# A new opening and first stage with projections one tile ahead, in a hybrid-mixer inference step

## The chip, the cores and the metric

One Trainium2 chip, one of its cores. The metric is the device time of one execution in microseconds; the kernel before takes 2571.53 us as the median of three runs (2570.34 to 2575.14). One execution was profiled: 2571.76 us of device time, of which the profile's span, from the first to the last instruction, covers 2569.9 us.

## What is computed

1024 latent and 256 context tokens of 1024 channels pass one layer: a modulated RMSNorm, an input projection of 56 column tiles of 128, three token mixers in parallel (Hyena long convolution, FNet, RG-LRU), a gated merge, an output projection, a second norm and a SwiGLU feed-forward. Cut to what the change touches:

```
mod = silu(c) @ w_ada + b_ada              # shift, scale, gate of both norms, for latent and context
h   = rmsnorm(x, n1) * (1 + sc1) + sh1
u   = h @ w_in                             # tiles: 12 Hyena, 4 FNet, then pairs (recurrent input, gate), 24 gates
k   = sin(freq * (sin(freq * (feats @ fw1 + fb1)) @ fw2 + fb2)) @ fw3 * decay     # Hyena filters, 8 chunks
kf  = rfft(k);   v, x1, x2 = depthwise_conv(u_hy, 3 taps)
xr  = depthwise_conv(u_rx, 4 taps)
r, i = sigmoid(xr @ w_r + b_r), sigmoid(xr @ w_i + b_i)     # per block of 128 channels, two directions
log_a = -8 * r * softplus(-lam);  h = scan(exp(log_a), sqrt(1 - a*a) * i * xr)
```

## The kernel before, in words

The program is written by hand for five engines, each with its own instruction list; semaphores order them. The order of the work is the order in each list. Activations lie with channels on the 128 partitions and the 1280 tokens along the free axis, in three pieces: 512 and 512 latent tokens, 256 context tokens. All products keep full precision: a weight tile is split by POOL into a rounded high part and a remainder (`split`, L798 and L801), `h` likewise into `h_hi` and `h_lo`, and `split_product` (L840 to L842) adds three products. One projection tile is 8 channel blocks x 3 pieces x 3 products into PSUM banks 0 to 2 (`projection_tile`). The other five banks, 3 to 7, are handed out in turn to all other products (`MixUnits`; `mix_done` and `mix_free` count them).

The stages that the change touches:

**Opening** (to the first projection). PE computes the filter network's two small layers (L893, L900) over 1280 positions, with 64 hidden channels. VectorE (DVE) takes each layer's argument into the range of the sine (`reduce_angle`, L1684 to L1688) and ScalarE (ACT) takes the sine (L1280, L1296). The second layer is computed twice, into both halves of the partitions (`h2f`). ACT squares the eight channel blocks of x (L1270), DVE sums them (L1677), and ones-products give the mean square of each token (L909); its inverse root goes onto diagonals (L1730) and is spread over the partitions by three more products (L917); DVE multiplies x by it (L1751). In between PE makes four rows of the modulation (`ada_row_unit`, L877, 16 products with 32 output channels each in four column groups), one after the other: each row is copied by ACT (L1288 and the line before it), turned into columns by PE (`ada_turn_unit`, L886) and added to its bias by DVE (L1736) before ACT may copy the next, since all share one buffer. DVE and ACT then make `h_hi` and `h_lo` block by block (L1785 to L1802), and PE's first projection waits for each block. The softplus of the decay parameters (three small parts on DVE, `softplus`, with an Exp and a Ln on ACT in between, L1275 and L1277) runs during the squares.

**First stage**: 16 projection tiles (12 Hyena, 4 FNet) and 8 filter chunks in eight passes (`l1_pass`; seven in a loop, the last apart). After `projection_tile(0)` and the filter taps of chunk 0 (`taps_units`, L945), pass i issues on PE: an ada row (L877), three products of the filter's spectrum (`fwd_unit`, L930) which wait for DVE's even part (`fa_ready`), projection tile 2i+1, a sum, three more spectrum products which wait for DVE's odd part, the turn, the taps of chunk i+1, and projection tile 2i+2. For each Hyena or FNet tile ACT writes a base (`conv_base`, L1331) and DVE adds two neighbours (`conv_sides`, L1814 to L1818) and frees the three banks. DVE further makes the taps (`make_taps`, L1853), their sums and the first stage of a transform (`first_stage`, L219 to L231).

**Second stage**: eight chunks of FNet and recurrent work. For chunk n PE issues projection tiles 16+2n and 17+2n, then waits for `xr_ready` and issues 12 products (L1023); ACT copies the first tile into the padded buffer `rin` (L1342), and DVE convolves it into `xr` (`conv_chunk`, L1828 and L1833), which also waits for that chunk's constants `rpack`. SP loads `rpack` of chunk 0 (L652) only after all eight filter chunks are stored (L643, L651).

SP issues every DMA from one list; `load_ahead(t, slot)` loads tile t+2 once tile t is split.

Of the kernel before, what the change touches and what calls it, by code (L numbers as in the profile page):

```python
# [14 lines left out]
P = 128  # L15
# [25 lines left out]
def u_made(n, by_act):  # L41
    return U_BY_ACT[:n + 1].count(by_act)

# [246 lines left out]
def build_program(nc, dr):  # L290

    ctx = ExitStack()
    with ctx:
# [11 lines left out]
        feats = sb(st, "feats", [FILT_EMB, T])  # L305
        h1f = sb(st, "h1f", [FILT_HID, T])
        arg, turns = sb(st, "arg", [P, T]), sb(st, "turns", [P, T])
# [24 lines left out]
        h2f = filt_ada[:, :]  # L332
# [17 lines left out]
        f_w2 = sb(st, "f_w2", [FILT_HID, P])  # L350
# [182 lines left out]
        FILT_UNIT = (0, 1, 2, 4, 5, 6)  # L533
        SQUARES_UNIT = 3
        ROW_UNIT = tuple(range(7, 7 + 2 * ROWS_FIRST, 2))
        TURN_UNIT = tuple(range(8, 8 + 2 * ROWS_FIRST, 2))
        u_setup = MixUnits([0] * MIX_BANKS, 6 + 1 + 2 * ROWS_FIRST)
# [50 lines left out]
        def _(sp):  # L588
# [37 lines left out]
            def l1_pass(i, last):  # L626
                load_ahead(2 * i, 0)
                if not last:

                    sp.wait_ge(taps_ready, i + 1)  # L630
                    load_taps(i + 1)
                sp.wait_ge(hy_conved, 2 * i + 2)
                sp.dma_start(dr["hy_s"][2 * i], hout[0][:]).then_inc(hy_stored[0], 16)
                load_ahead(2 * i + 1, 1)
                if not last:

                    sp.wait_ge(ada_row_ready, i + (ROWS_FIRST + 1))
                    for g in range(2):
                        sp.dma_start(ada_w[g][:], dr["w_ada"][2 * i + (ADA_FIRST + 2 + g)]).then_inc(ada_in[g], 16)
                sp.wait_ge(hy_conved, 2 * i + 3)  # L640
                sp.dma_start(dr["hy_s"][2 * i + 1], hout[1][:]).then_inc(hy_stored[1], 16)
# [193 lines left out]
        def _(pe):  # L835
# [53 lines left out]

            pe.wait_ge(filt1_in, 32)  # L890
            for j, (a, e, _) in enumerate(PIECES):
                out, done = mix_unit(u_setup, 0, FILT_UNIT[j])
                mm(out[0:FILT_HID, 0:e - a], f_w1[:, :], feats[:, a:e], start=True, stop=True).then_inc(done, 1)  # L893

            pe.wait_ge(consts_set, 3)
            pe.wait_ge(filt_in, 32)
            pe.wait_ge(sin_ready, 1)
            for j, (a, e, _) in enumerate(PIECES):
                out, done = mix_unit(u_setup, 0, FILT_UNIT[3 + j])
                mm(out[:, 0:e - a], f_w2[:, :], h1f[:, a:e], start=True, stop=True).then_inc(done, 1)  # L900
            pe.wait_ge(csilu_set, 2)
            pe.wait_ge(vec_in, 16)
            for r in range(ROWS_FIRST):
                ada_row_unit(u_setup, 0, ROW_UNIT[r], [2 * r, 2 * r + 1], 16)
                if r == 0:
                    out, done = mix_unit(u_setup, 0, SQUARES_UNIT)
                    pe.wait_ge(x_sq_summed, KD - 1)
                    for tile in range(NT):
                        ins = mm(out[:, 2 * tile:2 * tile + 2], x_sq_sum[:, tile * P:(tile + 1) * P], ones[:, 0:2],  # L909
                                 start=True, stop=True)  # L910
                    ins.then_inc(done, 1)
                ada_turn_unit(u_setup, 0, TURN_UNIT[r], r + 1, 0, 512)
                if r == 1:

                    pe.wait_ge(diag_ready, 1)
                    for b, (a, e, _) in enumerate(PIECES):
                        mm(ps[b][:, 0:e - a], ones[:],  # L917
                           rstd_diag[:, a // P:e // P, :].rearrange("p t m -> p (t m)"),
                           start=True, stop=True).then_inc(proj_done[b], 1)
# [15 lines left out]
            def taps_units(units, it, j0, loads):  # L935

                pe.wait_ge(w3_in, loads)
                for group in ((0, 1), (2, 3), (4,)):
                    banks_of = [mix_unit(units, it, j0 + j) for j in group]
                    for s in range(2):  # L940
                        for half, j in enumerate(group):
                            out, done = banks_of[half]
                            tile = 2 * j + s
                            rows = slice(half * FILT_HID, (half + 1) * FILT_HID)
                            ins = mm(out[:, s * 256:(s + 1) * 256], h2f[rows, tile * P:(tile + 1) * P], w3[rows, :],  # L945
# [4 lines left out]
            def l1_pass(i, units, it, last):  # L950
# [5 lines left out]
                projection_tile(2 * i + 1, 1)  # L956
# [54 lines left out]
            with pe.Fori(0, KD // 2) as m:  # L1011
                for s in range(2):
                    n = 2 * m + s
                    projection_tile(2 * n + L2_TILE0, 0)
# [10 lines left out]
                    if s == 0:  # L1025
                        fnet_channels(m)

# [206 lines left out]
        def _(act):  # L1234
# [19 lines left out]
            def take_filter(layer):  # L1254
                rows = P if layer else FILT_HID
# [4 lines left out]
                for j, (a, e, _) in enumerate(PIECES):  # L1260
                    src, free = take_mix(u_setup, 0, FILT_UNIT[3 * layer + j])
                    fn(arg[0:rows, a:e], src[0:rows, 0:e - a], ACT.Identity, bias=f_bias[0:rows, layer:layer + 1],
                       scale=f_vec[0:rows, 2:3]).then_inc(free, 1)

            for k in range(KD):
# [7 lines left out]
                if k == 3:  # L1273
                    act.wait_ge(sp_ready, 1)
                    fn(sp_w[:, 2, :], sp_w[:, 1, :], ACT.Exp).then_inc(sp_act, 1)  # L1275
                    act.wait_ge(sp_ready, 2)
                    fn(sp_w[:, 4, :], sp_w[:, 3, :], ACT.Ln).then_inc(sp_act, 1)  # L1277
                if k == KD - 3:
                    act.wait_ge(arg_ready, 1)
                    fn(h1f[:, :], arg[0:FILT_HID, :], ACT.Sin).then_inc(sin_ready, 1)  # L1280
            take_filter(1)
            act.wait_ge(consts_set, 3)
            for r in range(ROWS_FIRST):
                src, free = take_mix(u_setup, 0, ROW_UNIT[r])
                act.wait_ge(mod_ready, r)
                own(fn(ada_row[:, :], src[:, :], ACT.Copy))
                act.sem_inc(free, 1)
                act.sem_inc(ada_row_ready, 1)  # L1288
                if r == 0:
                    src, free = take_mix(u_setup, 0, SQUARES_UNIT)  # L1290
                    own(fn(rstd_col[:, :], src[:, 0:2 * NT], ACT.Sqrt, bias=eps[:, 0:1], scale=1.0 / D))
                    act.sem_inc(free, 1)
                    act.sem_inc(rms_ready, 1)
                if r == 1:
                    act.wait_ge(arg_ready, 2)
                    fn(h2f[:, :], arg[:, :], ACT.Sin).then_inc(sin_ready, 1)  # L1296
# [9 lines left out]
            act.wait_ge(proj_done[2], 1)  # L1306
            fn(rstd_ctx, ps[2][:, 0:CTX], ACT.Copy).then_inc(proj_free[2], 1)
# [48 lines left out]
            def l1_pass(i, units, it, last):  # L1356

                conv_base(2 * i, 0)
# [8 lines left out]
                conv_base(2 * i + 1, 1)  # L1367
# [10 lines left out]

            taps_squares(0)
# [4 lines left out]
            act.wait_ge(rin_zero, 1)  # L1384
# [988 lines left out]
```

## Time and profile before

| | us |
|---|---|
| median of three runs | 2571.53 |
| the profiled execution | 2571.76 |
| its span | 2569.9 |
| PE busy | 2479.5 (96%) |
| DVE busy | 1460.8 (57%) |
| POOL busy | 696.0 (27%) |
| ACT busy | 620.9 (24%) |

PE is TensorE's matmuls. A busy share is an average over the stages; the idle tenth of a stage has to be looked up where it stands. The granted clock is a mean of 0.983 over the span; 1.0 is 2.4 GHz and 0.5 is 1.2 GHz.

### The profile page before, as it was taken

What the parts mean: (1) busy time and instruction counts of PE and PEld (TensorE: products, weight loads), DVE (VectorE), ACT (ScalarE), POOL (GpSimd) and SP (SyncE); (2) the same over time, 40 slices, a digit from 0 to 9 for tenths busy, and PEclk for the clock granted to TensorE, in tenths of its full rate; (3) what the DMA queues carried; (4) which work ended last, traced back from release to release, by engine and by line L of the source; (5) the groups of instructions that cost most, each with busy time, mean ns of one, the idle gap of its engine ahead of it and who ended that gap; (6) DMA issues with size and microseconds to landing.
All of it is one profiled execution on the core that took longest, in us unless ns stands there. A gap on an engine that the chain in (4) does not pass through costs nothing. (4 is left out here: it accounts for less than half of the span.)

```text
span 2569.9 us, 34710 instructions
## 1 busy us (share of the span) xinstructions
PE 2479.5 (96%) x13478; PEld 2102.7 (82%) x13478; DVE 1460.8 (57%) x2697; ACT 620.9 (24%) x889; POOL 696.0 (27%) x300
## 2 busy tenths in 40 slices
PE   5799999999997999999999999999999999999997
PEld 2588888877876888888878878888888888888886
DVE  5878786678777676777763474633223322333236
ACT  4422222575753222222210012300000000000004
POOL 1011111223121222222333460442314331342220
PEclk8799999999998999999999999999999999999999
DMA  7244443111232222222453250111101010110002
GB/s 303 84 162 157 161 157 135 65 55 51 82 122 104 101 100 100 100 100 107 155 212 126 88 193 20 50 49 34 34 31 49 33 49 16 49 49 33 25 25 83
DMA packets 53755, 234.26 MB, mean 91 GB/s; under 512 B 6131, under 2 KB 8755, under 8 KB 48068
## 3 DMA queue, kind: packets, MB, share of 16 engines
q1 hardware_dynamic: 53700, 233.54, 25.2%
q8 instruction: 34, 0.56, 0.1%
q14 instruction: 21, 0.17, 0.0%
HBM read 178.98 MB, written 54.53 MB: 91 GB/s over the span
## 5 line engine op out<-in xcount | busy, mean ns | idle before, releaser
L840 PE MATMUL ps<-h_hi,w_hi 128*128 128x512 f32 (+1 forms) x2112 | 762.1, 361 | 13.5 <-DVE h_lo L1799 6.3
L841 PE MATMUL ps<-h_lo,w_hi 128*128 128x512 f32 (+1 forms) x2112 | 751.0, 356 | 0.0
L842 PE MATMUL ps<-h_hi,w_lo 128*128 128x512 f32 (+1 forms) x2112 | 750.9, 356 | 0.0
L798 POOL TENSOR_TENSOR w_hi<-w_raw,zero_col 128x1024 fp32r<-128x1024 f32 x96 | 206.4, 2150 | 1583.9 <-PE ps L842 1385.4
L840 PEld LDWEIGHTS ps<-h_hi,w_hi 128*128 128x128 f32 x2112 | 401.3, 190 | 78.8 <-issue 14.6
L842 PEld LDWEIGHTS ps<-h_hi,w_lo 128*128 128x128 f32 x2112 | 401.1, 190 | 57.1
L841 PEld LDWEIGHTS ps<-h_lo,w_hi 128*128 128x128 f32 x2112 | 401.5, 190 | 56.4 <-issue 0.2
L2151 DVE TENSOR_TENSOR a<-sil,ps 128x512 f32<-128x512 f32 (+1 forms) x66 | 39.5, 599 | 504.1 <-PE ps L842 501.7
L801 POOL TENSOR_TENSOR w_lo<-w_raw,w_hi 128x1024 fp32r<-128x1024 f32 x96 | 270.1, 2813 | 7.5
L2174 DVE SCALAR_TENSOR_TENSOR x<-ps,mod,x 128x512 f32<-128x512 f32 (+1 forms) x264 | 172.3, 661 | 98.1 <-PE ps L842 97.6
L841 PE MATMUL ps<-h_lo,wf_hi 128*128 128x512 f32 (+1 forms) x624 | 224.4, 360 | 0.0
L840 PE MATMUL ps<-h_hi,wf_hi 128*128 128x512 f32 (+1 forms) x624 | 223.1, 358 | 0.0
L842 PE MATMUL ps<-h_hi,wf_lo 128*128 128x512 f32 (+1 forms) x624 | 221.8, 355 | 0.0
L1568 ACT ACTIVATE sil<-ps 128x512 f32<-128x512 f32 (+1 forms) x66 | 34.7, 527 | 752.0 <-PE ps L842 751.8
L840 PE MATMUL ps<-act_hi,wf_hi 128*128 128x512 f32 (+1 forms) x528 | 187.2, 355 | 0.6 <-DVE act_lo L2157 0.6
L842 PE MATMUL ps<-act_hi,wf_lo 128*128 128x512 f32 (+1 forms) x528 | 186.9, 354 | 0.0
L841 PE MATMUL ps<-act_lo,wf_hi 128*128 128x512 f32 (+1 forms) x528 | 186.9, 354 | 0.0
L798 POOL TENSOR_TENSOR wf_hi<-w_raw,zero_col 128x1024 fp32r<-128x1024 f32 x48 | 94.8, 1974 | 181.2 <-PE ps L842 181.2
L840 PEld LDWEIGHTS ps<-h_hi,wf_hi 128*128 128x128 f32 x624 | 117.2, 188 | 20.4 <-issue 0.2
L841 PEld LDWEIGHTS ps<-h_lo,wf_hi 128*128 128x128 f32 x624 | 117.5, 188 | 18.3 <-issue 0.2
L842 PEld LDWEIGHTS ps<-h_hi,wf_lo 128*128 128x128 f32 x624 | 117.1, 188 | 18.6
L801 POOL TENSOR_TENSOR wf_lo<-w_raw,wf_hi 128x1024 fp32r<-128x1024 f32 x48 | 116.0, 2418 | 3.8
(277 smaller groups left out, 3506.2 us busy)
## 6 DMA issues: line engine op xcount, KB each, us to landing
w_raw<-in_weights SPq DMA_DIRECT2D x146, 512.0 KB, 3.5
ada_w<-in_w_ada SPq DMA_DIRECT2D x18, 1024.0 KB, 8.1
scratch_gate_s<-g_st SPq DMA_DIRECT2D x24, 640.0 KB, 3.3
side<-scratch_gate_s SPq DMA_DIRECT2D x24, 640.0 KB, 4.0
scratch_k_s<-kstage SPq DMA_DIRECT2D x8, 1536.0 KB, 6.6
hy_k<-scratch_k_s SPq DMA_DIRECT2D x8, 1536.0 KB, 8.5
scratch_hy_s<-hout SPq DMA_DIRECT2D x16, 640.0 KB, 3.2
ada_early<-in_w_ada SPq DMA_DIRECT2D x6, 1024.0 KB, 22.2
```

Source lines behind the costliest of these rows:

```text
L798: nc.gpsimd.tensor_tensor(hi[:], w_raw[slot % 2][:], zero_col[:].to_broadcast([P, D]), ALU.add).then_inc(pool_step, 1)
L801: nc.gpsimd.tensor_tensor(lo[:], w_raw[slot % 2][:], hi[:].bitcast(F32), ALU.subtract).then_inc(split_done, 1)
L840: mm(out, w_pair[0], x_pair[0], start=first, stop=False)
L841: mm(out, w_pair[0], x_pair[1], start=False, stop=False)
L842: return mm(out, w_pair[1], x_pair[0], start=False, stop=last)
L1568: fn(sil[n % 2][:, 0:e - a], ps[b][:, 0:e - a], ACT.Silu).then_inc(f_free[b], 1)
L2151: tt(a32[n % 2][:, 0:e - a], sil[n % 2][:, 0:e - a], ps[ub][:, 0:e - a], ALU.mult).then_inc(f_free[ub], 1)
L2174: stt(x1[:, m, a:e], ps[b][:, 0:e - a], mod[:, 5 * KD + m, seq:seq + 1], x1[:, m, a:e], ALU.mult, ALU.add).then_inc(f_free[b], 1)
```

## The change

- The filter network runs on 768 columns in place of 1280: the positions are put into two halves of the partitions (`HALF_TILES`: six tiles of 128 positions each, the two context tiles in both), so `h1f`, `arg`, `turns` and `h2f` shrink to 768 columns and use all 128 partitions. Each layer is two pieces (512 and 256) x two halves, a half to each 64 output partitions.
- In the opening's order DVE sums all squares first and reduces the first angle then; the mean-square products come ahead of the second layer. The four ada rows get a buffer each (`ada_rows`), the four turns share one bank, and one DVE addition takes all four. Two rows' products follow the spreading products, then two turns, the last row, two turns.
- The softplus moves from the opening to the end of the first stage, on DVE and on ACT.
- Projections of the first stage run one tile ahead: `projection_tile(1)` follows the taps of chunk 0, pass i computes tiles 2i+2 and 2i+3, and the last pass computes tile 16, the recurrent input of chunk 0, in its middle and none at its end. ACT copies it into `rin` there, after DVE has zeroed the edges there. Bases, sides, loads and stores move with their tiles; one store comes ahead of the passes.
- The second stage's first pair of chunks is written out ahead of its loop, without tile 16.

```diff
+HALF_TILES = ((0, 1, 4, 5, 8, 9), (2, 3, 6, 7, 8, 9))
+HALF_T = 6 * P
+HALF_PIECES = [(0, 512), (512, HALF_T)]
...
             def l1_pass(i, last):                                  # SP
-                load_ahead(2 * i, 0)
+                load_ahead(2 * i + 1, 1)
...
-                sp.wait_ge(hy_conved, 2 * i + 2)
-                sp.dma_start(dr["hy_s"][2 * i], hout[0][:]).then_inc(hy_stored[0], 16)
-                load_ahead(2 * i + 1, 1)
+                sp.wait_ge(hy_conved, 2 * i + 3)
+                sp.dma_start(dr["hy_s"][2 * i + 1], hout[1][:]).then_inc(hy_stored[1], 16)
                 if not last:
+                    load_ahead(2 * i + 2, 0)
...
             load_taps(0)
+            load_ahead(0, 0)
+            sp.wait_ge(hy_conved, 2)
+            sp.dma_start(dr["hy_s"][0], hout[0][:]).then_inc(hy_stored[0], 16)
...
+            def filter_layer(layer, w_at, rows_at):                # PE
+                for j, (a, e) in enumerate(HALF_PIECES):
+                    out, done = mix_unit(u_setup, 0, FILT_UNIT[2 * layer + j])
+                    for half in range(2):
+                        rows = slice(half * FILT_HID, (half + 1) * FILT_HID)
+                        ins = mm(out[rows, 0:e - a], w_at(rows), rows_at(half, rows, a, e), start=True, stop=True)
+                    ins.then_inc(done, 1)
...
+            filter_layer(1, lambda rows: f_w2[rows, :], lambda half, rows, a, e: h1f[rows, a:e])
+            row_product(0)
+            pe.wait_ge(diag_ready, 1)
...
+            row_product(1)
+            row_product(2)
+            row_turn(0)
+            row_turn(1)
+            row_product(3)
+            row_turn(2)
+            row_turn(3)
...
                 for j in range(3):                                 # PE, l1_pass
                     fwd_unit(units, it, 1 + j, range(4 * j, 4 * j + 4), False, f_a, fwd)
-                projection_tile(2 * i + 1, 1)
+                projection_tile(2 * i + 2, 0)
...
                     taps_units(units, it, 9, 16 * i + 32)
-                    projection_tile(2 * i + 2, 0)
+                    projection_tile(2 * i + 3, 1)
             projection_tile(0, 0, h_ready)
             taps_units(u_taps, 0, 0, 16)
+            projection_tile(1, 1)
...
-                    projection_tile(2 * n + L2_TILE0, 0)           # PE, l2_pair
+                    if not (first and s == 0):
+                        projection_tile(2 * n + L2_TILE0, 0)
...
-                conv_base(2 * i + 1, 1)                            # ACT, l1_pass
+                if not last:
+                    conv_base(2 * i + 2, 0)
+                else:
+                    act.wait_ge(rin_zero, 1)
+                    into_padded(L2_TILE0 + 1, rin)
...
+            for k in range(1, KD):                                 # DVE
+                sum_square(k)
             reduce_angle(0)
...
+            conv_sides(0, 0)
             make_taps(u_taps, 0, 0, 16)
             even_stage()
...
             l1_pass(7, u1_last, 0, True)
+            for part in range(3):
+                softplus(part)
```

## Rows read from the trace of the kernel before

**Rows 1.** Waits of PE: line, releaser, us in total, times, longest.
```profile
PE ps L930 <- DVEq L1897: 12.9, 1, 12.9
```

**Rows 2.** Timeline of PE: start, us, instructions, [idle before <- releaser].
```profile
28.77 4.60 PE L900 MATMUL ps<-h1f,f_w 64*128 64x512 f32 x6 [16.44 <-ACT h1f L1280]
...
39.02 1.86 PE L886 MATMUL ps<-vec,ada_row 128*128 128x2 f32 x8 [0.41 <-ACTq L1292]
40.82 3.64 PE L877 MATMUL ps<-ada_early,csilu 128*32 128x256 f32 x32
...
47.08 4.61 PE L917 MATMUL ps<-rstd_diag,ones 128*128 128x512 f32 x6
...
55.89 1.93 PE L877 MATMUL ps<-ada_early,csilu 128*32 128x256 f32 x32
58.75 1.02 PE L886 MATMUL ps<-vec,ada_row 128*128 128x2 f32 x8 [0.93 <-ACTq L1288]
63.94 0.76 PE L840 MATMUL ps<-h_hi,w_hi 128*128 128x512 f32 x1 [4.17 <-DVE h_lo L1799]
...
90.42 4.37 PE L945 MATMUL ps<-w,filt_ada 64*128 64x256 f32 x20 [1.01 <-DMA w<-in_w]
94.72 1.93 PE L877 MATMUL ps<-ada_w,csilu 128*32 128x256 f32 x32
109.56 6.84 PE L930 MATMUL ps<-f_a,fwd 128*128 128x128 f32 x40 [12.90 <-DVEq L1897]
...
154.46 4.73 PE L930 MATMUL ps<-f_a,fwd 128*128 128x128 f32 x40
```

**Rows 3.** Stretches: us, then PE, PEld, DVE, ACT, POOL busy, granted clock, DMA share, GB/s.
```profile
45.00:50.00 5.00, 4.62 (x12) 3.10 (x13) 0.99 (x3) 2.67 (x3) 4.92 (x3) 0.50 0.98 411
54.00:56.00 2.00, 1.07 (x12) 1.08 (x16) 0.05 (x2) 0.60 (x1) 0.00 (x0) 1.00 0.02 4
90.00:92.00 2.00, 1.57 (x8) 1.32 (x10) 0.00 (x0) 0.00 (x0) 0.00 (x0) 0.50 0.93 291
```

**Rows 4.** Timeline of DVE in the opening and the first passes.
```profile
12.53 1.49 DVE L1677 TENSOR_TENSOR x_sq_sum<-x_sq_sum,x_sq 128x1280 f32<-128x1280 f32 x1 [4.15 <-ACT x_sq L1270]
...
14.78 0.82 DVE L1684 TENSOR_SCALAR turns<-arg 64x1280 f32<-64x1280 f32 x1 [0.25 <-DVE sp_w L1698]
...
16.48 3.00 DVE L1687 SCALAR_TENSOR_TENSOR arg<-turns,arg 64x1280 f32<-64x1280 f32 x2
...
61.40 0.17 DVE L1736 TENSOR_TENSOR mod<-ps,vec 128x8 f32<-128x8 f32 x1
...
93.33 4.04 DVE L1853 TENSOR_TENSOR taps<-ps,decay 128x256 f32<-128x256 f32 x10 [4.98 <-DMA decay<-in_decay]
...
153.53 1.28 DVE L1814 SCALAR_TENSOR_TENSOR hout<-ps,vec,hout 128x1023 f32<-128x1023 f32 x1 [1.22 <-ACT hout L1335]
```

**Rows 5.** The tile x_in to 110 us: its DMAs (first and last start), time to landing.
```profile
L606 SPq DMA_DIRECT2D x_in<-in_x x7: 432/445/814, 4.1 to 7.6; - x7
...
DMA to landing us min/median/max: 6.4/9.9/13.1
```

**Rows 6.** Timeline at the end of the first stage: DVE and PE.
```profile
451.33 8.77 DVE L1833 SCALAR_TENSOR_TENSOR xr<-rin,rpack,xr 128x1024 f32<-128x1024 f32 x6
...
434.67 0.95 PE L886 MATMUL ps<-vec,ada_row 128*128 128x2 f32 x8
...
463.15 8.75 PE L1023 MATMUL ps<-xr,rpack 128*128 128x512 f32 x24
```

**Rows 7.** There: SP's issue, the landing of rpack's two loads, L1833's durations (ns).
```profile
441.12 0.34 SPq L652 DMA_DIRECT2D rpack<-in_rpack  x1
...
DMA to landing us min/median/max: 2.8/6.9/11.1
...
L1833 DVE SCALAR_TENSOR_TENSOR xr<-rin,rpack,xr x6: 472/1284/3302, 451.3 to 459.6; 128x1024 f32<-128x1024 f32 x3, 128x256 f32<-128x256 f32 x3
```

**Rows 8.** Timeline of POOL there.
```profile
453.19 2.89 POOL L798 TENSOR_TENSOR w_hi<-w_raw,zero_col 128x1024 fp32r<-128x1024 f32 x1 [18.76 <-DMA w_raw<-in_weights]
```

More of the change, by code:

```diff
@@ L890, in _ @@
             pe.wait_ge(filt1_in, 32)
-            for j, (a, e, _) in enumerate(PIECES):
-                out, done = mix_unit(u_setup, 0, FILT_UNIT[j])
-                mm(out[0:FILT_HID, 0:e - a], f_w1[:, :], feats[:, a:e], start=True, stop=True).then_inc(done, 1)
+            filter_layer(0, lambda rows: f_w1[:, :], lambda half, rows, a, e: feats[:, half * HALF_T + a:half * HALF_T + e])
             pe.wait_ge(consts_set, 3)
+            out, done = mix_unit(u_setup, 0, SQUARES_UNIT)
+            pe.wait_ge(x_sq_summed, KD - 1)
@@ L896, in _ @@
+            for tile in range(NT):
+                ins = mm(out[:, 2 * tile:2 * tile + 2], x_sq_sum[:, tile * P:(tile + 1) * P], ones[:, 0:2],
+                         start=True, stop=True)
+            ins.then_inc(done, 1)
             pe.wait_ge(filt_in, 32)
             pe.wait_ge(sin_ready, 1)
-            for j, (a, e, _) in enumerate(PIECES):
-                out, done = mix_unit(u_setup, 0, FILT_UNIT[3 + j])
-                mm(out[:, 0:e - a], f_w2[:, :], h1f[:, a:e], start=True, stop=True).then_inc(done, 1)
+            filter_layer(1, lambda rows: f_w2[rows, :], lambda half, rows, a, e: h1f[rows, a:e])
@@ L1259, in take_filter, with take_row @@
                 act.wait_ge(f_bias_set, 1)
[L1260 to L1263, printed above, removed]
+                for j, (a, e) in enumerate(HALF_PIECES):
+                    src, free = take_mix(u_setup, 0, FILT_UNIT[2 * layer + j])
+                    fn(arg[:, a:e], src[:, 0:e - a], ACT.Identity, bias=f_bias[:, layer:layer + 1],
+                       scale=f_vec[:, 2:3]).then_inc(free, 1)
+            def take_row(r):
+                src, free = take_mix(u_setup, 0, ROW_UNIT[r])
+                own(fn(ada_rows[r][:, :], src[:, :], ACT.Copy))
+                act.sem_inc(free, 1)
+                act.sem_inc(ada_row_ready, 1)
             for k in range(KD):
@@ L1406, in take_fnet_tokens, with l2_pair @@
                     fn(dst, src, ACT.Copy).then_inc(free, 1)
-            with act.Fori(0, KD // 2) as m:
+            def l2_pair(m, first):
                 for s in range(2):
                     n = 2 * m + s
-                    act.wait_ge(xr_ready, n + 1)
-                    into_padded(2 * n + (L2_TILE0 + 1), rin)
+                    if not (first and s == 0):
+                        act.wait_ge(xr_ready, n + 1)
+                        into_padded(2 * n + (L2_TILE0 + 1), rin)
                     if s == 1:
@@ L1679, in reduce_angle @@
             def reduce_angle(layer):
-                rows = P if layer else FILT_HID
-                for j in range(3):
-                    mix_taken(u_setup, 0, FILT_UNIT[3 * layer + j])
-                x, n = arg[0:rows, :], turns[0:rows, :]
+                for j in range(2):
+                    mix_taken(u_setup, 0, FILT_UNIT[2 * layer + j])
+                x, n = arg[:, :], turns[:, :]
                 own(ts(n, x, 1.0 / (2 * math.pi), ROUND, ALU.mult, ALU.add))
@@ L1873, in l1_pass @@
                 dve.sem_inc(fa_ready, 1)
-                conv_sides(2 * i + 1, 1)
+                if not last:
+                    conv_sides(2 * i + 2, 0)
+                else:
+                    zero_edges()
                 ada_add(units, it, 8, 2 * i + ADA_FIRST, 4)
@@ L1879, in l1_pass, with zero_edges @@
                 own.restart()
+            def zero_edges():
+                for a, e in ((0, PAD_LAT), (PAD_LAT + LAT, PAD_CTX), (PAD_CTX + CTX, PAD_T)):
+                    own(nc.vector.memset(rin[:, a:e], 0.0))
+                dve.sem_inc(rin_zero, 1)
             def sum_squares(i):
```

162 lines of the change are left out of this document (78 added, 84 removed).

## Prediction

> **What bounds the kernel now.** The page first: PE is busy for 96% of the span, so time can be won only where PE stands still, or where its work waits in a chain of other engines. The waits of PE come next. In the whole first stage there is one wait for another engine, 12.9 us for DVE's even part before the first pass [rows 1]; in the passes that follow PE never waits. The timeline of PE [rows 2] shows the rest: 16.4 us of idle before the filter's second layer at 28.8, small products in a chain of copies to 59.8, 4.2 us of idle, and the first projection at 63.94. What ended last before that projection is the chain row product, ACT copy, turn, DVE addition (61.40, [rows 4]), the norm's scale, `h_hi`, `h_lo`. From there to 89.2 PE is fed block by block by DVE, and that pace is not changed. So there are three places: the path to 63.94, the hole before 109.56, and the passage to the second stage, where today PE goes from the last turn through tiles 16 and 17 to 463.15 [rows 6] with no wait in that view.
>
> **The change part by part: the opening.** x decides its head. The last of its loads is issued at 7.6 and may land 13.1 us later [rows 5], at 20.7. The DVE sums, undisturbed by angle and softplus, follow the loads: one square, about 1.3 us (the 1280-column sine and square are alike), and one sum, 1.49 [rows 4], give 23.5; the sum chain by itself, 12.53 + 7 x 1.49 = 23.0, is no later. The angle on 768 columns: the three scalar instructions fall from 0.82 to about 0.55 and the two fused ones from 1.5 to about 0.95 [rows 4], scaled with 0.15 us fixed each, 3.5 in all: 27.0. ACT's table load lies ahead of its wait, as the opening's others do. The sine, about 0.8, gives 28.0, with one hop 28.2. Before, the second layer began at 28.77: doing the angle last costs nothing, because the sums end 9 us earlier.
>
> The second layer took 4.60 us for 1280 columns [rows 2], 3.6 ns each. After, it has 512 + 256 columns for each of two halves. Side by side the halves cost 768 x 3.6 = 2.8 us, one after another 5.5. Nearest is the row of the taps: 10 products of 256 columns on alternating 64-row halves took 4.37 us [rows 2], 1.7 ns a column, and half of that lies at a granted clock of 0.50 [rows 3]: halves overlap there. I take 2.8: 31.0. The squares' products (2.4 us) lie in PE's idle time before the sine, and their root, on ACT right after the sine, gives the diagonals at 31.5.
>
> The Trainium skill, in "TensorEngine Tiling (Array Packing)", Restrictions and Gotchas, says that different row tiles can't use one PSUM bank at the same time. The taps' halves go to two banks and the new layer's two halves to one, so by the page this layer takes 5.5 us; no row of this trace has two row halves on one bank.
>
> Row product 0 follows: 3.0 at the low clock, 34.0. The three spreading products, 4.61 [rows 2]: 38.6. DVE scales two pieces from 36 to 46, beside this. Then PE has rows 1 and 2, turns 0 and 1, row 3, turns 2 and 3, and waits for no copy: a buffer each, and turns 0 to 2 have another product between copy and use. The last turn's copy hides behind turn 2. The cost hangs on the clock. The granted clock was 0.50 from 45 to 50 and 1.00 at 54 [rows 3]; the full 128x128 spreading products lay in between. After that a row took 1.93 and a turn 1.02, before it 3.64 and 1.86 [rows 2]. I take the same here, the clock rising behind the spreading products: 2.4 + 1.9 + 2 x 1.0 + 1.9 + 2 x 1.0 and 0.3 of hops = 10.5, so 49.1. From the addition to the first projection passed 63.94 - 61.40 = 2.54: 51.7, against 63.94. Gain 12.2. At the low clock throughout it is 3 x 3.6 + 4 x 1.86 = 18.2 and 59.4: gain 4.6. The weights' split on POOL (42 to 51) now overlaps DVE's scaling, which reads PSUM; the same pair overlapped before without slowing, so nothing. Ada loads landed by 41 and row 3 starts at 45.
>
> **The first stage.** In the old clock, from 89.2. `conv_sides(0)` now goes ahead of `make_taps` on DVE. It takes 3.5 us and starts at 90.0, when the base is made; make_taps began at 93.33, held by the decay's load [rows 4], so it is moved by 0.3 at most. Bank release at 93.6 comes before the taps' end at 94.8. PE then has tile 1: a tile is 13.8 us (435.6 to 463.15 for tiles 16 and 17, [rows 6], halved), to 108.6, and the ada row, 1.93, to 110.5, where today it stands still until 109.56. DVE's even part is ready at 109.8. So PE no longer waits, and the spectrum products, at a clock that has not fallen, take 4.73 and not 6.84 [rows 2]: tile 2 starts at 115.3 where tile 1 started at 116.15. A whole tile is done for nothing and 0.8 us are gained besides. Should the clock stay low for the tile's first 5 us, 2.5 us go.
>
> In the passes tile, base, sides, loads, stores and splits move by one tile together, and each engine has the same order as before. DVE keeps its room: in pass 1 it waits 1.22 us for ACT's base [rows 4], and PE takes the even part 2 us after it was made (154.46, [rows 2]). Nothing is gained or lost. The loads, stores and the wait for the second conv move on SP's queue in the same step; the store put ahead of the passes costs one issue of 0.3, and no tile waits for it. In the last pass tile 16 takes the place of 15; zeroing the edges, 0.3 us, lies in DVE's idle time.
>
> **The passage.** PE ends the last turn at 435.5 [rows 6] and now has only tile 17, to 449.3. Before, tiles 16 and 17 hid the making of xr. `rin` is filled by 430. The softplus on DVE and ACT starts at 435.9 and needs two table loads of 1.28 and some 3 us of small instructions: done by 440.8, with k_scale. What comes last is rpack: issued 441.12, once the last filter chunk is stored, and landed 2.8 us later [rows 7], at 443.9. The softplus is hidden with 3 us to spare. conv_chunk(0) took 10.1 us, its two largest parts drawn out to 3.3 and 2.1 us against 1.28 and 0.47 [rows 7], when POOL split tile 18 (453.19, [rows 8]). It now lies before that split, and undisturbed is 1.17 + 3 x 1.77 = 6.5: xr at 450.5. With the wait, PE starts the 12 products at 450.7, 1.4 us of new idle, where before it was 463.15 [rows 6]. With the 0.8 from the first pass, which moves the whole chain: gain 13.2.
>
> The FNet's first stage on DVE is late next: its input lands at 451.8, it takes 4, and POOL's split now falls on it, costing by the loss above up to 3.7: 459.5, and PE ends the 12 products (8.75, [rows 6]) at 459.4. So 0 to 2 us. The Trainium skill, in "SBUF — State Buffer", Who interferes with whom, has the pair as a lock held for a whole instruction; the rows agree in kind (3.3 and 2.1 us), and by it DVE could lose both of POOL's instructions, 5.3 us, and PE 1.7. Later stages are ordered by PE and don't change.
>
> **The sum.** 12.2 + 13.2 = 25.4 us off the profiled execution's own 2571.76 (span 2569.9 and 1.9 around it), which lies 0.2 above the median of 2571.53: 2546.3. I add 0.7 for the FNet stage: **2547**.
>
> **The rivals.** A. The two halves of the layer run one after another: 2.7 us more, 2550. For it: two row halves on one bank, which no row shows. B. The clock does not rise behind the spreading products, since the rows around them use few columns: 7.6 us more, 2554.5. For it: the second layer's 4.60 us did not raise it before. Against: one run of spreading products did. C. The passage is later than worked out: rpack lands late, or DVE meets a split: 3.7 to 5 us more, 2551. D. The extra tile waits for the sides behind DVE, or tile 16's place frees nothing: the hole stays and only the opening gains, 2571.8 - 12.2 = 2559.5; the change would not do what it says, but the bank's release before the taps' end speaks against it. E. Slower: in every pass DVE's sums and transform meet a split by POOL that now falls elsewhere. Each split costs DVE 3.7 us by the rows; two a pass are 7.4, less the room of 2.0, 5.4 over eight passes 43: 2547 + 43 = 2590. It decides from a delay of 5.1 us a pass on (25 / 8 + 2.0). Against it: POOL's split waits for the tile's end in both orders, so it stays where it was.
>
> **How the numbers follow.** Forecast 0.47, A 0.17, B 0.13, C 0.12, D 0.05, E 0.03, and 0.03 for no change to speak of. The first four, with 2543 to 2549 for the forecast's own spread, hold 0.89; a range from 2543 to 2557 takes B in and leaves out D, E and the tails, about 2 in 10. A change under 0.2% (5.1 us) can't be told from none here. Faster 0.93, same 0.04, slower 0.03.
>
> **What would show it.** First projection near 51.7 and PE's clock at 1.00 by 42; the second layer at 2.8 us; no wait of PE for L1897's successor, and tile 1 right behind the taps; one wait of 1 to 2 us before the 12 products, with rpack as what came last for DVE; L1833 without a 3.3. The prediction is wrong if PE's first projection is later than 58, or if waits of PE turn up inside the passes.

## The result, and the profile after

| | us |
|---|---|
| before, median of 4 runs | 2570.94 (2570.18 to 2575.14) |
| after, median of 4 runs | 2552.05 (2550.76 to 2560.04) |
| ratio | 0.9929, 95% interval 0.9916 to 0.9942 |
| after, the profiled execution | 2560.04, span 2558.2 |

The change is worth 18 to 19 us, 0.7%. 2547 was forecast, with a range of 2543 to 2557. The profiled execution after is the slowest of its four; a second profile of the same kernel, below, has a span of 2551.6. So this first profile shows larger losses than the second.

The timeline of PE after. The first seven lines answer to the opening [rows 2], the next two to the first pass, the last two to the passage [rows 6].

```profile
25.61 4.40 PE L929 MATMUL ps<-ones,x_sq_sum 128*128 128x2 f32 x20 [13.81 <-DVE x_sq_sum L1727]
30.09 2.82 PE L904 MATMUL ps<-h1f,f_w 64*64 64x512 f32 x8
32.84 2.74 PE L885 MATMUL ps<-ada_w,csilu 128*32 128x256 f32 x32
35.51 2.42 PE L942 MATMUL ps<-rstd_diag,ones 128*128 128x512 f32 x6
37.86 3.66 PE L885 MATMUL ps<-ada_early,csilu 128*32 128x256 f32 x64
45.19 1.96 PE L917 MATMUL ps<-vec,ada_row 128*128 128x2 f32 x16
53.19 0.76 PE L848 MATMUL ps<-h_hi,w_hi 128*128 128x512 f32 x1 [6.04 <-DVE h_lo L1846]
...
79.62 5.49 PE L979 MATMUL ps<-w,filt_ada 64*128 64x256 f32 x20 [1.49 <-DMA w<-in_w]
...
102.81 4.73 PE L963 MATMUL ps<-f_a,fwd 128*128 128x128 f32 x40
...
441.31 8.86 PE L1060 MATMUL ps<-xr,rpack 128*128 128x512 f32 x24 [0.62 <-DVEq L1883]
455.03 10.19 PE L1029 MATMUL ps<-fn_ch,fn_a 128*128 128x256 f32 x32 [4.86 <-issue]
```

The last line's products in the kernel before, from its timeline of PE, right behind the 12 products and without a wait:

```profile
471.74 7.07 PE L994 MATMUL ps<-fn_ch,fn_a 128*128 128x256 f32 x32
```

Read it by its shifts. The first projection comes 10.7 us earlier (63.94 to 53.19). The 12 recurrent products come 21.8 us earlier (463.15 to 441.31), with the hole of 12.9 us gone and a wait of only 0.6 us in the passage. Then, within one step, 4.9 us of idle ahead of the FNet products, and these take 10.2 us where they took 7.1: of 21.8 us 13.6 are left. The span is 11.7 us shorter, so some 2 us more go later: PE's waits at the output projection (the releasers now L2118 and L2127) are 8.4 us together against 6.2.

DVE and POOL side by side show what both losses are. First the timeline of DVE after, at the norm's start and in the passage:

```profile
42.34 4.87 DVE L1791 TENSOR_TENSOR x_in<-x_in,ps 128x512 f32<-128x512 f32 x8 [0.21 <-DVE x_in L1791]
47.43 0.19 DVE L1797 TENSOR_TENSOR mod<-ps,vec 128x32 f32<-128x32 f32 x1 [0.22 <-DVE x_in L1791]
47.86 1.96 DVE L1805 SCALAR_TENSOR_TENSOR norm_a<-mod,vec 128x8 f32<-128x8 f32 x2 [0.24 <-DVE mod L1797]
49.97 2.34 DVE L1832 TENSOR_SCALAR u_t<-x_in,norm_a,mod 128x512 f32<-128x512 f32 x1 [0.16 <-DVE norm_a L1805]
...
434.91 1.14 DVE L1875 TENSOR_SCALAR xr<-rin,rpack 128x1024 f32<-128x1024 f32 x2 [3.02 <-DMA rpack<-in_rpack]
436.09 5.11 DVE L1880 SCALAR_TENSOR_TENSOR xr<-rin,rpack,xr 128x1024 f32<-128x1024 f32 x6
...
444.34 2.18 DVE L226 TENSOR_TENSOR fn_a<-fn_c 128x128 f32<-128x128 f32 x2
...
446.78 2.44 DVE L226 TENSOR_TENSOR fn_c<-fn_c 128x128 f32<-128x128 f32 x1
449.14 1.98 DVE L223 TENSOR_TENSOR fn_c<-fn_c 128x128 f32<-128x128 f32 x1
...
451.24 2.43 DVE L226 TENSOR_TENSOR fn_a<-fn_c 128x128 f32<-128x128 f32 x1
...
454.61 0.28 DVE L226 TENSOR_TENSOR fn_a<-fn_u 128x128 f32<-128x128 f32 x1
```

and the timeline of POOL after, in the same places:

```profile
43.41 1.89 POOL L806 TENSOR_TENSOR w_hi<-w_raw,zero_col 128x1024 fp32r<-128x1024 f32 x1 [42.15 <-DMA w_raw<-in_weights]
...
47.70 1.89 POOL L806 TENSOR_TENSOR w_hi<-w_raw,zero_col 128x1024 fp32r<-128x1024 f32 x1
49.67 2.36 POOL L809 TENSOR_TENSOR w_lo<-w_raw,w_hi 128x1024 fp32r<-128x1024 f32 x1
...
444.40 1.97 POOL L806 TENSOR_TENSOR w_hi<-w_raw,zero_col 128x1024 fp32r<-128x1024 f32 x1 [39.15 <-DMA w_raw<-in_weights]
446.45 2.62 POOL L809 TENSOR_TENSOR w_lo<-w_raw,w_hi 128x1024 fp32r<-128x1024 f32 x1
449.04 1.94 POOL L806 TENSOR_TENSOR w_hi<-w_raw,zero_col 128x1024 fp32r<-128x1024 f32 x1
451.05 2.48 POOL L809 TENSOR_TENSOR w_lo<-w_raw,w_hi 128x1024 fp32r<-128x1024 f32 x1
```

A DVE instruction of 0.28 us, of which the transform is made, ends when the POOL instruction that ran beside it ends: 446.78 + 2.44 is 449.22, and POOL's ends at 449.07. So it goes with one per POOL instruction, four in a row here (one of the two at 444.34 is the first), since tiles 18 and 19 are split back to back; the four lose 7.7 us together. At the norm's start two instructions, one of the `norm_a` pair and the first `u_t`, lose 3.4 us together. "Issue" in PE's line looks like no fetch of code: DVE's last FNet instruction ends at 454.9 and PE starts at 455.03; `fnet_free` below tests it.

The clock, in stretches of the kernel after (columns as in [rows 3]): low under the first row product, low from within the wait before the first projection, low again behind tile 0, and low over the first 6 us of the FNet products.

```profile
32.00:34.00 2.00, 2.00 (x18) 0.68 (x18) 1.96 (x3) 1.33 (x2) 0.00 (x0) 1.00 1.01 422
47.00:53.00 6.00, 0.14 (x2) 0.06 (x1) 5.31 (x6) 2.93 (x4) 4.95 (x3) 0.60 0.73 301
85.00:89.00 4.00, 4.00 (x10) 3.14 (x10) 3.50 (x8) 1.57 (x1) 2.51 (x2) 0.50 0.50 158
455.00:466.00 11.00, 10.97 (x37) 9.10 (x38) 9.20 (x7) 10.94 (x12) 0.00 (x0) 0.72 0.11 40
```

The first line needs care. It reads 1.00, but the row product runs at the pace of 3.64 us for 32 products until about 34.5 and at that of 1.93 [rows 2] only from there on: 8 products in the half microsecond from 33.5 and 16 in that from 34.5. The reading is 1.00 in both, so this early in the trace the durations tell the clock and the reading doesn't.

### The profile page after: what moved, and what is told of

The parts are those of the page before. It is cut to its first block and busy times, and to the rows that moved or that the text cites. A ratio compares the mean times of both kernels' runs of the same rounds, so it can differ in the third digit from the quotient of the medians.

```text
span 2558.2 us, 34628 instructions
## 1 busy us (share of the span) xinstructions
PE 2473.3 (97%) x13482; PEld 2099.4 (82%) x13482; DVE 1465.8 (57%) x2694; ACT 617.2 (24%) x886; POOL 696.4 (27%) x300
## 3 DMA queue, kind: packets, MB, share of 16 engines
q1 hardware_dynamic: 53764, 233.55, 25.4%
```

## The experiments

Each kernel was timed beside the kernel before on the same chip (median of before there: 2571.4 to 2571.8). The first four kernels ran on one chip, `after_again`, `both_free`, `warm` and `all_three` on a second, and `both_free_b`, `hold3`, `hold3_warm` and `softplus_back` on a third; kernels of one chip are best compared with each other.

**The two halves of the change.** `open_only` is the changed kernel with the passes, the loads and stores and the second stage's loop as before. `stage_only` is the other half on the old opening.

```diff
-                projection_tile(2 * i + 2, 0)      # open_only, each of these put back
+                projection_tile(2 * i + 1, 1)
...
+                projection_tile(2 * i + 2, 0)      # stage_only, each of these taken over
-                projection_tile(2 * i + 1, 1)
```

> The changed kernel with its first stage and passage put back as before: only the new opening (and the softplus at the end of the first stage) is left. Theory: the first projection starts near 53, not 64, PE ends tile 0 near 78, and all after that is shifted by the same 11 us, since DVE and PE keep their order: 2571 - 11 = 2560 (2558 to 2562), with the wait of PE for DVE's even part of 12 to 13 us still there. Rival: something later stands on the clock of the loads and not on PE, so that the opening's gain is given back in part: 2563 or more, with a longer wait before the first pass.

Measured: 2560.70 us, ratio 0.9964 (0.9950 to 0.9977). The hole is still there, from the timeline of PE:

```profile
98.34 6.59 PE L960 MATMUL ps<-f_a,fwd 128*128 128x128 f32 x40 [9.99 <-DVEq L1925]
```

The opening is worth 10.9 us. The hole is 10.0 and not 12.9, for the taps and the row product behind them ran at the low clock (5.49 and 3.64 us where they took 4.37 and 1.93) and filled some of it; the rival's delay did not come.

> The kernel before with only the first stage's projections one tile ahead, tile 16 in the last pass and the second stage's first pair written out; the opening is the old one. Theory: a tile's 13.8 us go into the old wait before the first pass, and the passage gives back a few: the 12 products at 463 - 12 = 451. Then the FNet's first stage on DVE meets two splits of POOL (tiles 18 and 19) and PE waits about 5 us and runs 3 us slower for the clock: 2571 - 12 + 8 = 2567 where the meeting is as in the profiled execution of the changed kernel; where the unprofiled ones escape it, 2559. Rival: the passage gains nothing at all, 2571.

Measured: 2564.99 us, ratio 0.9974 (0.9965 to 0.9983), 6.6 us less than before. From its timeline of PE:

```profile
111.56 4.73 PE L933 MATMUL ps<-f_a,fwd 128*128 128x128 f32 x40 [0.39 <-DVEq L1925]
...
449.91 8.86 PE L1029 MATMUL ps<-xr,rpack 128*128 128x512 f32 x24 [0.52 <-DVEq L1855]
462.54 8.83 PE L998 MATMUL ps<-fn_ch,fn_a 128*128 128x256 f32 x32 [3.77 <-issue]
```

The hole is filled and the 12 products come 13.2 us earlier, the size forecast for this part, though not from the terms forecast: the wait before them is 0.5 us in place of 1.4, and the 0.8 us that the first pass should have gained did not come. The step behind them takes back 3.8 us of idle and 1.8 of clock. 10.9 + 6.6 = 17.5 us against 17.7 and 18.9 for the whole by its two medians: the halves add up within the scatter, and each has its own loss.

**POOL's split at the norm.**

```diff
             split(0, 0, w_hi[0], w_lo[0])
+            pool.wait_ge(h_ready, 3 * KD)
             split(1, 1, w_hi[1], w_lo[1])
```

> The changed kernel, but POOL splits tile 1's weights only after the whole norm is done (it waits for h_lo's last block), in place of during the norm's first instructions. Theory: norm_a (1.96 us for two where it was 0.37) and the first u_t (2.34 where it was 0.55) were held by POOL's two instructions at 47.7 and 49.7; without them the first projection starts 3.4 us earlier, at about 50, and the whole runs 3 to 3.5 us shorter than the changed kernel (2552), 2548.5. Tile 1's split ends near 78 and its projection starts at 82: no new wait. Rival: their length is the clock of DVE's own chain (scalar operands just written) and not POOL: same start as before, 2552, both instructions still 1.9 and 2.3 us.

Measured: 2549.74 us (2546.61 to 2553.91). From the timeline of DVE:

```profile
47.61 0.37 DVE L1806 SCALAR_TENSOR_TENSOR norm_a<-mod,vec 128x8 f32<-128x8 f32 x2 [0.24 <-DVE mod L1798]
48.13 0.55 DVE L1833 TENSOR_SCALAR u_t<-x_in,norm_a,mod 128x512 f32<-128x512 f32 x1 [0.16 <-DVE norm_a L1806]
```

and PE's first projection, from its timeline:

```profile
49.86 0.80 PE L849 MATMUL ps<-h_hi,w_hi 128*128 128x512 f32 x1 [3.08 <-DMA fwd<-in_fwd]
```

The `norm_a` pair is back at 0.37 us and `u_t` at 0.55, and the projection starts 3.3 us earlier: it was POOL. (The releaser named in PE's line is not what it waited for: DVE's first `h_lo` ends at 49.7.) The runs scatter by 7 us, so the median's 2.3 us under the changed kernel say less than these lines.

**POOL's split at the FNet stage.** The loop over the tiles is cut at tile 18.

```diff
-            with pool.Fori(1, OUT_TILE0 // 2 + 1) as m:
+            with pool.Fori(1, L2_TILE0 // 2 + 1) as m:
...
+            pool.wait_ge(fna_ready, 1)
+            with pool.Fori(L2_TILE0 // 2 + 1, OUT_TILE0 // 2 + 1) as m:
```

> The changed kernel, but POOL splits tile 18 only when DVE has finished the first FNet stage (it waits for fna_ready once). Theory: the stage's small instructions took 2.0 to 2.4 us each in place of 0.28 while POOL split tiles 18 and 19 back to back; without that the stage ends near 445 and PE goes on from the 12 products without its 4.9 us of idle and without the low clock after it (10.2 us for the FNet products where they had been 7.1): the profiled execution is 8 us shorter than the changed kernel's own, 2552 in place of 2560; the median falls by 0 to 8 us, by how often the other executions met the same. Rival: the 4.9 us, which the waits call issue, are the fetch of the written-out code: the idle stays and nothing is gained.

Measured: 2549.12 us (2547.06 to 2550.75), the profiled execution 2549.93. From the timeline of PE:

```profile
440.94 8.86 PE L1066 MATMUL ps<-xr,rpack 128*128 128x512 f32 x24 [0.42 <-DVEq L1889]
449.64 7.07 PE L1035 MATMUL ps<-fn_ch,fn_a 128*128 128x256 f32 x32
```

Idle and slow products are both gone, 8.0 us in all, and the FNet products end at 456.7 and not 465.2, while the written-out code is still there: the rival falls. The median is only 2.9 us under the changed kernel's, with intervals that overlap (0.9905 to 0.9932 against 0.9916 to 0.9942). That the changed kernel's other executions lose less here is the likely reason; their traces were not taken, but the second profile, next, does lose less.

**The changed kernel again.**

> The changed kernel itself, unaltered, beside the others on one chip. Its profiled execution lay 8 us above the median of its other three (2560.0 against 2551.3). Theory: the profiled one met the worst of the clock at the FNet products (10.2 us for what takes 7.1) and after; a second profile has the same wait of 3 to 5 us there, and lies between 2550 and 2560; median 2552. Rival: profiled executions of this kernel are always 8 us longer: 2560 again in the profile, 2551 in the median.

Measured: 2554.08 us (2548.28 to 2556.05), profiled 2553.36. Its timeline of PE has:

```profile
99.79 4.73 PE L963 MATMUL ps<-f_a,fwd 128*128 128x128 f32 x40 [0.51 <-DVEq L1953]
...
450.67 8.83 PE L1029 MATMUL ps<-fn_ch,fn_a 128*128 128x256 f32 x32 [3.48 <-issue]
```

The same wait, 3.5 us and not 4.9, and 8.8 us of products and not 10.2. So the wait belongs to the kernel and its size to the execution; that profiled ones are always longer is refuted. `split1_late` and `softplus_back`, which leave this place alone, lose least: waits of 3.1 and 3.2 us, and products of 7.14.

**Both of POOL's moves.** The edits of split1_late and fnet_free together.

> The changed kernel with both of POOL's moves: tile 1 is split after the norm, tile 18 after the first FNet stage. Theory: the two are at different places on the path, so the gains add: first projection near 50, no idle before the FNet products; 2552 - 2.3 - 2.9 by the medians measured for each alone = 2547, or 2552 - 3.4 - 4.9 = 2544 by the traces. Rival: they share a cause, or the freed time is lost at the next clock change: 2549.

Measured: 2546.22 us beside after_again's 2554.08, ratio 0.9900 (0.9886 to 0.9915): 7.9 us, where the expectation had 5.2 by the medians and 8.3 by the traces. It is at the theory's place and not at the rival's 2549. But one line was new, from the timeline of PE:

```profile
99.30 6.32 PE L970 MATMUL ps<-f_a,fwd 128*128 128x128 f32 x40 [3.70 <-DVEq L1960]
```

The same kernel was run once more, on another chip:

> The kernel of both POOL moves once more, as the one that the next two are read against on this chip. 2546 (2543 to 2549). In its profile PE waits 0 to 4 us for DVE's even part before the first pass: the two runs of the kernel differ there by when tile 1 ends, which sets when POOL splits tile 3.

Measured: 2543.66 us (2542.70 to 2546.13). This time the products start without a wait, at 97.96. What differs is the clock behind tile 0. The taps of `both_free`, then those of `both_free_b`, from their timelines of PE:

```profile
76.40 2.85 PE L986 MATMUL ps<-w,filt_ada 64*128 64x256 f32 x20 [0.97 <-DMA w<-in_w]
```

```profile
76.94 5.21 PE L986 MATMUL ps<-w,filt_ada 64*128 64x256 f32 x20 [1.00 <-DMA w<-in_w]
```

With fast taps tile 1 ends early and POOL splits tile 3 from 93.9 on, beside DVE's even part, two of whose instructions then take 1.99 and 2.42 us; with slow ones the split comes at 96.3, when the even part is done.

**Products added to hold the clock.** 14 products of 512 columns into a free bank, in the last piece of tile 0 and behind it.

```diff
+                    fill = made is not None and b == 2
+                    if fill:
+                        spare = u_taps.bank(4)
+                        pe.wait_ge(mix_free[spare], u_taps.nth(0, 4))
                     for k, (w, x) in enumerate(zip(ws, xs)):
+                        if fill:
+                            mm(mix(spare), xs[0][0][:, 0:P], xs[0][0][:, 0:512], start=True, stop=True)
...
                     ins.then_inc(proj_done[b], 1)
+                    if fill:
+                        for _ in range(6):
+                            mm(mix(spare), xs[0][0][:, 0:P], xs[0][0][:, 0:512], start=True, stop=True)
```

> The changed kernel with 14 products of 512 columns added on PE whose result nothing reads, one ahead of each block of tile 0's last piece and six behind it, where PE waits for DVE and for the taps' constants. Theory: the granted clock fell to 0.50 behind tile 0 because PE stood still in between; kept busy it stays at 1.00, the taps take about 3 us and not 5.5, tile 1 starts 2.6 us earlier (with DVE's release of the banks, near 82.4) and loses none of its first 4 us; the spectrum products start near 99 in place of 102.8, when DVE's even part is ready: 3 to 4 us shorter than the changed kernel. Rival: the added products delay tile 0's own by their length, and the clock falls all the same: 0 to 2 us longer.

Measured: 2558.65 us, 4.6 us longer than after_again. From its timeline of PE:

```profile
79.54 2.85 PE L988 MATMUL ps<-w,filt_ada 64*128 64x256 f32 x20
102.16 7.17 PE L972 MATMUL ps<-f_a,fwd 128*128 128x128 f32 x40 [3.88 <-DVEq L1962]
```

then of DVE:

```profile
96.64 1.99 DVE L226 TENSOR_TENSOR f_a<-f_t 128x128 f32<-128x128 f32 x1
98.76 2.42 DVE L226 TENSOR_TENSOR f_a<-f_t 128x128 f32<-128x128 f32 x1
```

and of POOL:

```profile
96.59 1.90 POOL L806 TENSOR_TENSOR w_hi<-w_raw,zero_col 128x1024 fp32r<-128x1024 f32 x1 [8.79 <-PE ps L850]
98.56 2.47 POOL L809 TENSOR_TENSOR w_lo<-w_raw,w_hi 128x1024 fp32r<-128x1024 f32 x1
```

The clock was high: the granted clock is 1.00 from 62 to 93 and the taps take 2.85 us. They do so in all three profiles with the added products, and in two of the nine without them and with the new opening (`both_free` and `hold3`; 4.45 to 5.49 us in the other seven). So the added products seem to hold the clock, but one trace would not show it. The gain turned into a loss. Tile 1 ended earlier, so POOL split tile 3 earlier, on top of DVE's even part; PE waited 3.9 us, its clock fell after all, and the products took 7.2 us. Neither theory nor rival had this. The 12 products of the passage start 4.5 us later than in `after_again` (442.80 against 438.33). In this profile the FNet step was also at its worst (5.5 us of idle, 9.7 of products).

> The changed kernel with both of POOL's moves and the 14 added products. Theory: the three act at three places and add up: 2552 - 5 to 8 - 3.5 = 2540 to 2543, 1.1% under the kernel before. Rival: the clock falls at another place instead, and it is as both_free.

Measured: 2547.37 us beside both_free's 2546.22: the sum did not come. Its trace has the same meeting, a wait of 3.8 us before the first pass's products.

**Tile 3's split held too.** On both moves, and then with the added products:

```diff
+            pool.wait_ge(proj_done[2], 2)
+            split(2, 0, w_hi[0], w_lo[0])
+            pool.wait_ge(fa_ready, 1)
+            pool.wait_ge(proj_done[2], 3)
+            split(3, 1, w_hi[1], w_lo[1])
+            with pool.Fori(2, L2_TILE0 // 2 + 1) as m:
```

> Both POOL moves, and POOL splits tile 3 only when DVE's even part for the first pass is made. Theory: where PE is early with tile 1, the split of tile 3 meets DVE's even part and holds two of its instructions for 1.99 and 2.42 us in place of 0.28, so PE waits 3.7 us, its clock falls and the spectrum products take 6.3 in place of 4.7. Without the meeting the products start at 95.6 where they started at 99.3, and take 4.7: 5 us shorter than both_free in the profile, 2541 to 2543 in the median. Rival: DVE's even part is simply longer than tile 1, and the wait stays: 2546.

Measured: 2543.02 us (2541.12 to 2543.71). The products start at 95.95 with no wait and take 4.73, as expected:

```profile
95.95 4.73 PE L975 MATMUL ps<-f_a,fwd 128*128 128x128 f32 x40
```

Its taps took 2.85 us, as those of `both_free` did, and there the products started at 99.30 and took 6.32: at the same clock the held split is worth 4.9 us up to their end. But `both_free_b`, its partner on the chip, had slow taps, did not meet the split either, and is slower by only 0.6 us in the medians. The traces show the mechanism; that holding the split pays on average is not shown.

> As hold3, with the 14 added products that keep PE busy behind tile 0. Theory: the added products did what they were for (clock 1.00 and taps of 2.85 us in place of 5.5), and lost it again because the earlier end of tile 1 let POOL's split of tile 3 meet DVE; with that split held, they are worth 0 to 3 us: no longer than hold3, 2540 to 2543, and steadier, with the taps at 2.85 in the profile. Rival: the added products cost by themselves: 1 us or more above hold3.

Measured: 2541.26 us (2540.52 to 2543.81), ratio 0.9887 (0.9872 to 0.9902). The taps take 2.85 us. With tile 3's split held, the added products no longer cost 4.6 us; 1.8 us under hold3 is within both kernels' scatter, and since the profile of hold3 had fast taps too, the two traces show no gain of theirs. Nor is it steadier: its runs span 3.3 us, those of hold3 2.6. It has the lowest median of all, 0.4% under the changed kernel by the two ratios.

**The softplus back in the opening.** ACT's Exp and Ln move with DVE's parts.

```diff
-            for k in range(1, KD):
-                sum_square(k)
+            sum_square(1)
+            softplus(0)
+            sum_square(2)
+            softplus(1)
+            for k in range(3, KD):
+                sum_square(k)
+                if k == 4:
+                    softplus(2)
```

> The changed kernel with the softplus back in the opening, its parts put between the sums of the squares. Theory: in the opening it lies on DVE's path to the first angle (some 3 us of small instructions and ACT's two table loads between squares), at the end of the first stage it was hidden under the load of rpack: the first projection starts 1 to 3 us later, and the whole is 1 to 3 us longer than the changed kernel, 2554 to 2556. Rival: the sums wait for ACT's squares anyway and have room for it: same as the changed kernel, 2552 to 2554.

Measured: 2549.87 us (2548.89 to 2553.37), not longer than the changed kernel. From its timeline of DVE:

```profile
28.08 0.55 DVE L1733 TENSOR_SCALAR turns<-arg 128x768 f32<-128x768 f32 x1
...
50.55 1.01 DVE L1811 SCALAR_TENSOR_TENSOR norm_a<-mod,vec 128x8 f32<-128x8 f32 x2 [0.24 <-DVE mod L1803]
```

and from that of PE:

```profile
53.42 0.76 PE L848 MATMUL ps<-h_hi,w_hi 128*128 128x512 f32 x1 [3.73 <-DVE h_lo L1852]
```

The first angle starts 2.7 us later than in the changed kernel's first profile (25.38), the norm's scale too (50.55 against 47.86), and the first projection only 0.2 us later (0.7 than in `after_again`). The time is lost, but it falls where POOL's split lies anyway: that ends at 51.3 here, so only `norm_a` is held, for 0.6 us in place of the 3.4 us before, and `u_t` takes 0.55. That is a third reason, beside theory and rival: moving the softplus buys almost nothing while POOL's split stands there. What it would buy with the split held was not tested.

## Why the prediction was right, and where it was off

The direction, the three places and the mechanism of the gain were right, and 2552 lies in the range. The forecast was 5 us too low, outside its own spread of 2543 to 2549. The range reaches 2552 because it was widened to 2557 for rival B, which did not come: that part is luck. Step by step:

- **Head of the opening.** Expected 28.2 for the second layer, measured 30.09. The sums end at 25.4 and not 23.5: the loads arrived in time, but two buffers tie ACT's square (1.27) to DVE's sum (1.49), 1.6 us a block, and in this execution the first block came 1.2 us later.
- **The layer's two halves** (rival A): 2.82 us, where 2.8 was expected. The row product behind it starts at the slow pace, and takes from 2.59 to 3.27 us in eight profiles of the new opening by when the clock rises in it, while the layer takes 2.82 or 2.83 in all; so the layer lay at the low clock, where one half after the other would take 5.5, and the halves of one bank ran side by side. The Trainium skill's page "TensorEngine Tiling (Array Packing)", Restrictions and Gotchas, is not borne out for this form; the measurement decides.
- **Rows and turns** (rival B): the clock rose even ahead of the spreading products, which took 2.42 us and not 4.61. The modulation was complete at 47.4, expected 49.1. B falls. This made up for the head.
- **From there to the projection**: 2.54 us were taken over from the old trace, measured 5.8. The step said that POOL's split beside DVE's scaling costs nothing, which held, but the scaling ended at 47.2 and the split ran to 52.0, over the norm's first instructions. The step's own times, 49.1 for the addition and 51 for the split's end, already overlapped there. This term was mis-sized by 3.2 us, and `split1_late` gives them back: 2.7 us from the addition to the projection.
- **The hole**: filled in every profile that has the new first stage, with a wait of at most 0.5 us left, but for the three variants in which tile 3's split came in (3.7 to 3.9 us). The clock's part went the way of the caution: tile 1 began at 0.50, the taps took 5.49 us, and the spectrum products start at 102.8, against an expected 98.3 (110.5 - 12.2): 1.5 from the opening, 3 from the clock. In the second profile the taps took 4.45 and the products start at 99.8.
- **The passage**: rpack issued at 431.9 and last, as expected; conv 6.3 us undisturbed (6.5 expected); wait 0.6 us (1.4 expected); softplus hidden.
- **The FNet stage**: expected 0 to 2 us, taken at 0.7. Measured 3.5 and 4.9 us of idle and 1.8 and 3.1 of low clock. One split was counted. There are two, because tile 17 is now done at 440.7, before tile 18's weights have landed for POOL (444.40), and nothing holds tile 19's split back; before, it waited for tile 17's end, behind the 453.19 of [rows 8]:

```profile
463.48 2.57 POOL L798 TENSOR_TENSOR w_hi<-w_raw,zero_col 128x1024 fp32r<-128x1024 f32 x1 [4.86 <-PE ps L842]
```

  By the step's own price of 3.7 us a split, two give 451.8 + 4 + 7.4 = 463.2 against 459.4 for PE, 3.8 us of idle, near the 3.5 and 4.9 measured; the low clock behind the idle was left out altogether. The rule of the Trainium skill's "SBUF — State Buffer", Who interferes with whom, that the loser is blocked for the whole instruction, fits all of these lines (2.34 beside 2.36, 2.44 beside 2.62); the prediction had applied it to one split.

Two mis-sized terms of the same kind, 3.2 and 3 to 8 us, and one for the clock, up to 3 us, stand against a faster row chain and passage. By the second profile, whose span lies 6.5 us above the forecast's (2551.6 against 2547 - 1.9): the 12 products start 0.6 us later than forecast (438.33 against 463.15 - 25.4), the FNet stage costs 5.2 us in place of 0.7, and some 1.5 us go at the output projection. B and D did not come. C came in part: DVE met a split and PE stood still for 3.5 and 4.9 us, about the 3.7 to 5 that it priced, but one step later than it said, behind the 12 products, and rpack was on time. E's mechanism, POOL's split meeting DVE, is what cost most here, only in single places and not in every pass: after the first pass PE waits for no DVE part until the passage.

Open: why the executions of the changed kernel differ by up to 9 us among themselves (the FNet stage, at 3 to 8 us, and the clock behind tile 0 vary between profiles, but what sets them was not tested), and the 1.5 to 2 us at the output projection in both profiles, which no experiment touched.

## What to carry to other kernels

When work is moved earlier, look up what it now runs beside. Here three of POOL's splits came to lie on DVE's critical instructions: at the norm, where the split stayed (46.47 before, 47.70 after) and the chain moved onto it; at the FNet stage, where both moved; and, in some executions, at the first pass, where an earlier end of tile 1 brought the split forward. A wait of one engine may be put on purpose (hold the split until the critical chain has passed): two such waits are worth 7.9 us here, more than the 6.6 us of the half of the change that reordered the first stage. A third wait and the added products lower the median by 2.4 us more, within the scatter of the runs (2543.66 to 2541.26 on one chip). And a chain is sized by the slowest neighbour that it may meet, not by its durations in a trace where it met none.

## What the runs showed of the hardware that was not expected

At the places above, DVE instructions with all operands in SBUF that meet a POOL elementwise instruction last until it ends (0.28 becomes 1.98 to 2.44 us, 0.55 becomes 2.34), and one or more get through between two POOL instructions. It can also go the other way: in the kernel before, POOL's instruction at 463.48 took 2.57 us, where others take 1.89, and the three of DVE's beside it kept their 0.28. Those that read PSUM are not held: DVE's scaling of x_in took 4.87 us for the eight from 42.34, beside the split from 43.41 on, and 4.86 for the eight from 37.27, with no split beside them. Behind waits of 3.5 to 5.5 us PE's products ran slow (6.3, 6.4 and 7.2 us in place of 4.73; 8.8, 9.7 and 10.2 in place of 7.07), at a granted clock of 0.50 (455 to 461 in the kernel after, 102.2 to 107 in `warm`). Such a stall cost 1.6 to 3.1 us beyond itself. But not every one does: behind waits of 3.1 and 3.2 us the FNet products took 7.14.
